# Two sets of recurrence scratch tiles, and channel chains issued in alternation

## The chip, the cores and the metric

The kernel runs on the 8 cores of one Trainium2 chip, one batch element per core, with no exchange between cores. Each core has five engines that take their own instruction streams in order and meet at semaphores: TensorE (PE), VectorE (DVE), ScalarE (ACT), GpSimd (POOL) and SyncE (SP, here only DMA issue). The metric is the device time of the slowest core in microseconds.

## The reference, cut to what matters

One hybrid decoder layer on x (8, 4096, 1024), float32. The change lies in the recurrent half of the mixer, `rg_lru` with the convolution before it:

```python
h = rms_norm(x, norm_mix)
x_rnn, gate_rnn, q, k, v = split(h @ w_in)           # 512 columns each
x_rnn = causal_depthwise_conv(x_rnn, conv_w, conv_b)  # width 4
r = sigmoid(einsum('bshi,hij->bshj', xh, w_a) + b_a)  # xh: x_rnn in 8 heads of 64
i = sigmoid(einsum('bshi,hij->bshj', xh, w_x) + b_x)
a = exp(-8 * r * softplus(-lam))
b = sqrt(1 - a * a) * (i * x_rnn)
hidden[t] = a[t] * hidden[t - 1] + b[t]               # scan over the sequence
y_rnn = hidden * gelu(gate_rnn)
y_sb = stick_breaking_attention(q, k, v)              # causal, 8 heads of 64
x = x + concat(rms_norm(y_rnn), rms_norm(y_sb)) @ w_out
```

After it come a cross-attention into 256 memory tokens and a mixture of 16 experts; the change does not touch them.

## The kernel before

**Stages.** The program has three stages with a barrier between them: the mixer (to about 2890 us), the cross-attention and the experts. Only the mixer's code changes.

**Tiles.** The mixer works on 8 query tiles of 512 tokens. For each tile `front_ops(qt)` (line 477) norms and transposes the tokens into `hT`, projects them with `w_in` in ten blocks of 256 columns (q, k, v, gate, and last blocks 0 and 1, the recurrence's input), and runs the recurrence. `attention(qt)` (line 590) goes through 8 heads times the key blocks of 128 up to the tile, one *item* each: 32 items for tile 0, 64 for tile 1, up to 256 for tile 7. `back_ops(qt)` (line 559) norms the attention output and applies `w_out`.

**An attention item.** Its steps are pipelined by hand: `s0` computes the scores Z of item t+2 on TensorE, `s1` takes e = exp(Z) and sp = ln(e + 1) of item t+1 on ScalarE, `s3` adds two matmuls to Z of item t (with the triangle `negU` on sp, and with `negOnes` on R, the running sum of the sp before) and lets VectorE update R with sp, `s4` takes w = exp(Z) on ScalarE, `s5` multiplies w of item t-1 with V. There are 3 buffers for Z (PSUM), sp and w. So each item's last matmul needs VectorE's R update of the item before, and w needs that matmul.

**What sets the order.** `front_ops` and `back_ops` only record their instructions (`Defer`, line 243). `attention(qt)` then issues, behind each item's steps, an equal share of a side list: `back_ops(qt - 1)`, `front_ops(qt + 1)` and six weight conversions by DMA (lines 670 to 673). With 35 steps in tile 0 and 259 in tile 7, that is about 11.7 side instructions a step in tile 0 and 2.3 in tile 6. `front_ops(0)` is issued alone ahead of everything. Every engine takes its instructions strictly in the order issued.

**A chain.** Each of blocks 0 and 1 holds two *chains* of 128 channels (lines 517 to 551), four per front, c = 0 to 3, one behind the other. A chain has 37 instructions: 8 matmuls into a PSUM bank, the convolution on VectorE (halo copy from `hal`, copy `xrt`, one tensor_scalar and three scalar_tensor_tensor into `xc`, halo saved, cast `xcb`), a matmul and a sigmoid for r, a matmul and a sigmoid for the input gate `ig`, then b and a by exponentials and a logarithm on ScalarE, two products, the scan with its state in `hst`, the product with the gate `gg`, the square `sq`, a matmul with ones, and the addition into `rstdF`. The sigmoid of the fronts 0 to 3 is three ScalarE passes; that of the fronts 4 to 7 is one ScalarE pass, an addition and a reciprocal on VectorE (`sigmoid_from`, line 468).

**Buffers.** All four chains use the same scratch tiles `xrt`, `xc`, `r_`, `ig`, `b_`, `xcb` (lines 408 to 410). The PSUM banks of the small matmuls and projections come in turn from `pmR`, two banks: within a chain they alternate, so that the two gate matmuls go to different banks. `xhR` has 3 buffers for the residual tokens that `back_ops` loads (line 580), adds to (line 585) and stores (line 586); load and store stand in SyncE's queue in this order, item by item.

## Time and profile before

| | us |
|---|---|
| median of 6 runs (5534.08 to 5628.45) | 5574.36 |
| the profiled execution | 5532.07 |
| its span on the slowest core | 5530.6 |
| ScalarE busy in the span | 2856.0 |
| TensorE busy (matmuls) | 3750.5 |
| VectorE busy | 2039.6 |

The page of the profile gives shares over the whole program, which mixes three stages with different limits. The change is in the first, so the rows below are cut from that stage: busy time of each engine by stretch, the timeline of single instructions, and who waited for whom. In a stretch, the span less an engine's busy time is its idle time. In a timeline row the first number is the start, the second how long it took; "x3" means that three like instructions are merged, from the first start to the last end.

### The profile page before, as it was taken

The numbers are of one execution on the slowest core, as the hardware profiler recorded it, in microseconds if no ns is written. First come the engines' busy times: TensorE is split into PE (matmuls) and PEld (weight loads), VectorE is DVE, ScalarE is ACT, GpSimd is POOL, SyncE is SP. The second block draws the span as 40 slices with busy tenths as digits, with TensorE's granted clock in tenths as the row PEclk, the third lists the DMA queues.
The fourth block names the chain that finished last, engine by engine and source line by source line (L and its number), as shares of the span: only waits on it lengthen the run. The fifth ranks groups of instructions, "written<-read, shape, count | busy, mean of one in ns | idle before, by whom it ended". The sixth has DMA issues, their size and how long they took to land. (4 is left out here: it accounts for less than half of the span.)

```text
span 5530.6 us, 64662 instructions; the slowest of 8 cores (5509.6 to 5530.6 us)
## 1 busy us (share of the span) xinstructions
PE 3750.5 (68%) x16080; PEld 1509.3 (27%) x16080; DVE 2039.6 (37%) x4139; ACT 2856.0 (52%) x5222; POOL 469.4 (8%) x463
## 2 busy tenths in 40 slices
PE   3545656667577667665544656647887977879798
PEld 1212222223122122211112222213333333333343
DVE  4434343443633633532222333333333333333332
ACT  2546676768788889889952232212323233232322
POOL 1000000000000000000000000001121111211121
PEclk8767778879789789889986767668999999999999
DMA  5634333422223122100224212123343243432443
GB/s 78 82 64 59 77 46 69 54 56 33 35 62 43 20 62 35 20 5 12 39 61 94 80 58 84 54 93 125 137 146 135 82 156 128 143 134 82 156 139 118
DMA packets 245839, 436.01 MB, mean 79 GB/s; under 512 B 15088, under 2 KB 146160, under 8 KB 245488
## 3 DMA queue, kind: packets, MB, share of 16 engines
q1 hardware_dynamic: 102672, 339.29, 18.3%
q0 software_dynamic: 142816, 92.59, 13.7%
q8 instruction: 153, 2.51, 0.2%
q14 instruction: 198, 1.62, 0.1%
HBM read 474.07 MB, written 75.50 MB: 99 GB/s over the span
## 5 line engine op out<-in xcount | busy, mean ns | idle before, releaser
L181 ACT ACTIVATE sp_u<-e__u,cst_u 128x512 bf16<-128x512 f32 (+3 forms) x1152 | 790.4, 686 | 166.8 <-ACT e__u L181 5.9
L184 PE MATMUL Z_u<-qT_u,KT_u 128*128 128x512 bf16 (+3 forms) x1152 | 456.9, 397 | 598.6 <-ACT w_u L181 590.2
L197 DVE TENSOR_TENSOR R_u<-R_u,sp_u 128x512 bf16<-128x512 bf16 (+2 forms) x1088 | 433.3, 398 | 1134.8 <-PE Z_u L184 1079.3
L181 ACT ACTIVATE w_u<-Z_u 128x512 bf16<-128x512 f32 (+3 forms) x1152 | 629.4, 546 | 250.7 <-PE Z_u L184 248.1
L181 ACT ACTIVATE e__u<-Z_u 128x512 f32<-128x512 f32 (+3 forms) x1152 | 636.3, 552 | 20.4 <-PE Z_u L184 20.2
L184 PE MATMUL g_u<-tT_u,wg_u 128*128 128x512 bf16 x2048 | 536.4, 403 | 137.2 <-DMA wg_u<-wg_s 84.9
L181 ACT ACT_TABLE_LOAD x212 | 272.0, 1283 | 604.0 <-DVE rt_u L201 215.4
L184 PE MATMUL u_u<-tT_u,wu_u 128*128 128x512 bf16 x2048 | 522.8, 397 | 2.1
L184 PE MATMUL Z_u<-R_u,negOnes_u 128*128 128x512 bf16 (+1 forms) x1088 | 446.5, 410 | 62.6 <-DVE R_u L197 62.6
L184 PE MATMUL Z_u<-sp_u,negU_u 128*128 128x512 bf16 (+3 forms) x1152 | 462.2, 401 | 15.6 <-ACT sp_u L181 15.3
L184 PE MATMUL dn_u<-wd_u,hid_u 128*128 128x512 bf16 x2048 | 455.9, 381 | 21.8 <-DVE hid_u L197 17.6
L184 PE MATMUL O_u<-w_u,V_u 128*128 128x512 bf16 (+3 forms) x1152 | 460.2, 400 | 6.8 <-ACT w_u L181 1.9
L197 DVE TENSOR_TENSOR hid_u<-u_u,sg_u 128x512 bf16<-128x512 f32 x256 | 177.1, 692 | 675.6 <-POOL sg_u L197 504.4
L181 ACT ACTIVATE sg_u<-g_u 128x512 f32<-128x512 f32 x256 | 152.6, 597 | 519.0 <-PE g_u L184 484.0
L197 POOL TENSOR_TENSOR sg_u<-sg_u,cb_u 128x512 f32<-128x512 f32 x256 | 295.3, 1154 | 1440.5 <-ACT sg_u L181 1401.3
L184 PEld LDWEIGHTS Z_u<-qT_u,KT_u 128*128 128x128 bf16 x1152 | 114.2, 99 | 1028.0 <-issue 1015.8
L188 PE MATMUL pT_u<-ident_u,hn_u 128*128 128x128 bf16 x784 | 147.1, 273 | 355.6 <-DVE hn_u L208 336.9
L184 PEld LDWEIGHTS g_u<-tT_u,wg_u 128*128 128x128 bf16 x2048 | 194.6, 101 | 387.9 <-issue 201.4
L184 PE MATMUL pm_u<-hT_u,win_u 128*128 128x512 bf16 x1024 | 295.2, 408 | 2.1 <-DVE hT_u L194 2.0
L184 PEld LDWEIGHTS u_u<-tT_u,wu_u 128*128 128x128 bf16 x2048 | 202.2, 102 | 250.0 <-issue 48.8
L184 PEld LDWEIGHTS dn_u<-wd_u,hid_u 128*128 128x128 bf16 x2048 | 192.8, 98 | 255.2 <-issue 36.3
L188 PEld LDWEIGHTS pT_u<-ident_u,hn_u 128*128 128x128 bf16 x784 | 79.3, 120 | 478.0 <-issue 465.4
(159 smaller groups left out, 4158.0 us busy)
## 6 DMA issues: line engine op xcount, KB each, us to landing
wg_u<-wg_s SPq DMA_DIRECT2D x128, 512.0 KB, 3.8
wu_u<-wu_s SPq DMA_DIRECT2D x128, 512.0 KB, 5.1
wd_u<-wd_s SPq DMA_DIRECT2D x128, 512.0 KB, 6.0
win_u<-w_in POOLq DMA_DIRECT2D x80, 512.0 KB, 7.5
xs_u<-x SPq DMA_DIRECT2D x32, 512.0 KB, 4.2
xh_u<-x SPq DMA_DIRECT2D x64, 256.0 KB, 3.6
wo_u<-w_out POOLq DMA_DIRECT2D x16, 1024.0 KB, 25.0
x1s<-xh_u SPq DMA_DIRECT2D x64, 256.0 KB, 2.5
```

The lines of the kernel that those rows point to most:

```text
L181: self.S.op("act", lambda e: e.activation(out=out, in_=in_, func=func, **kw), reads, writes)
L184: self.S.op("pe", lambda e: e.matmul(out, lhsT=lhsT, rhs=rhs, start=start, stop=stop, skip_group_check=skip), reads, writes, inc=inc)
L188: self.S.op("pe", lambda e: e.transpose(out=out, in_=in_, identity=ident), reads, writes, inc=inc)
L197: self.S.op(eng, lambda e: e.tensor_tensor(out=out, in0=in0, in1=in1, op=op), reads, writes)
```

## The change

The scratch tiles get a second set (`LT`, two dictionaries of tiles), and to make room `xhR` falls from 3 buffers to 2. The marks that order the accesses to `hal` and `hst` are kept per chain rather than one for all. The chain's code moves into a function `lru_chain`, which takes a set of scratch tiles and one PSUM bank and uses this bank for all its matmuls. For blocks 0 and 1, `front_ops` records the two chains of the block in two lists, one with each set and bank, and then appends their instructions in alternation. Each chain has the same 37 instructions as before, the side list is as long as before, and all that stands ahead of and behind the chains keeps its place in it.

```diff
@@ -403,13 +403,20 @@
             winR = Rot([sb("win%d" % i, [128, 8, 256], BF16) for i in range(4)], "win")
             woR = Rot([sb("wo%d" % i, [128, 8, 512], BF16) for i in range(2)], "wo")
             xsR = Rot([sb("xs%d" % i, [128, D], F32) for i in range(2)], "xs")
-            xhR = Rot([sb("xh%d" % i, [128, 512], F32) for i in range(3)], "xh")
+            xhR = Rot([sb("xh%d" % i, [128, 512], F32) for i in range(2)], "xh")
             t512 = lambda n, d, c: Rot([sb("%s%d" % (n, i), [128, 512], d) for i in range(c)], n)
-            xrt = sb("xrt", [128, 515], F32)
-            xc, r_, ig, b_ = [sb(n, [128, 512], F32) for n in ("xc", "r_", "ig", "b_")]
-            xcb = sb("xcb", [128, 512], BF16)
+            LT = []
+            for i in range(2):
+                T = {"xrt": sb("xrt%d" % i, [128, 515], F32), "xcb": sb("xcb%d" % i, [128, 512], BF16)}
+                for n_ in ("xc", "r_", "ig", "b_"):
+                    T[n_] = sb("%s%d" % (n_, i), [128, 512], F32)
+                for n_ in ("xrtB", "xcB", "rB", "igB", "bB", "xcbB"):
+                    T[n_] = Buf("%s%d" % (n_, i))
+                LT.append(T)
             e_ = sb("e_", [128, 512], F32)
-            xrtB, xcB, rB, igB, bB, xcbB, eB = [Buf(n) for n in ("xrt", "xc", "r", "ig", "b", "xcb", "e")]
+            eB = Buf("e")
+            halBs = [Buf("hal%d" % i) for i in range(4)]
+            hstBs = [Buf("hst%d" % i) for i in range(4)]
             sqR = t512("sq", BF16, 2)
             spR = t512("sp", BF16, 3)
             wR = t512("w", BF16, 3)
@@ -425,8 +432,8 @@
-            k.memset("pool", hal[:], 0.0, [halB])
-            k.memset("pool", hst[:], 0.0, [hstB])
+            k.memset("pool", hal[:], 0.0, halBs)
+            k.memset("pool", hst[:], 0.0, hstBs)
@@ -473,6 +480,45 @@
+
+            def lru_chain(kk, qt, c, wt, wtB, lo, T, bank, yTt, yTB):
+                pa, paB = bank
+                for dc in range(8):
+                    kk.mm(pa[:, :], wt[:, dc, lo:lo + 128], hT[:, dc, :], dc == 0, dc == 7,
+                          [wtB, hTB], [paB], inc=(dc == 7))
+                kk.copy("dve", T["xrt"][:, 0:3], hal[:, c, 0:3], [halBs[c]], [T["xrtB"]])
+                kk.copy("dve", T["xrt"][:, 3:515], pa[:, :], [paB], [T["xrtB"]])
+                kk.ts("dve", T["xc"][:], T["xrt"][:, 0:512], pp[:, c * 4:c * 4 + 1], pp[:, 16 + c:17 + c],
+                     ALU.mult, ALU.add, [T["xrtB"], ppB], [T["xcB"]])
+                for t in range(1, 4):
+                    kk.stt(T["xc"][:], T["xrt"][:, t:t + 512], pp[:, c * 4 + t:c * 4 + t + 1], T["xc"][:],
+                          ALU.mult, ALU.add, [T["xrtB"], ppB, T["xcB"]], [T["xcB"]])
+                kk.copy("dve", hal[:, c, 0:3], T["xrt"][:, 512:515], [T["xrtB"]], [halBs[c]])
+                kk.copy("dve", T["xcb"][:], T["xc"][:], [T["xcB"]], [T["xcbB"]])
+                pg, pgB = bank
+                kk.mm(pg[:, :], wbd[:, c, :], T["xcb"][:], True, True, [wbdB, T["xcbB"]], [pgB], inc=True)
+                sigmoid_from(kk, T["r_"], T["rB"], pg, pgB, c12[:, 12 + c:13 + c], on_act=(qt <= 3))
+                pg2, pg2B = bank
+                kk.mm(pg2[:, :], wbd[:, 4 + c, :], T["xcb"][:], True, True, [wbdB, T["xcbB"]], [pg2B], inc=True)
+                sigmoid_from(kk, T["ig"], T["igB"], pg2, pg2B, c12[:, 16 + c:17 + c], on_act=(qt <= 3))
+                kk.act(T["b_"][:], T["r_"][:], AF.Exp, [T["rB"], constB], [T["bB"]], scale=c12[:, 8 + c:9 + c])
+                kk.act(T["r_"][:], T["r_"][:], AF.Exp, [T["rB"], constB], [T["rB"]], scale=c12[:, 4 + c:5 + c])
+                kk.ts("dve", T["b_"][:], T["b_"][:], -1.0, 1.0, ALU.mult, ALU.add, [T["bB"]], [T["bB"]])
+                kk.act(T["b_"][:], T["b_"][:], AF.Ln, [T["bB"], constB], [T["bB"]], bias=cst[:, 1:2])
+                kk.act(T["b_"][:], T["b_"][:], AF.Exp, [T["bB"]], [T["bB"]], scale=0.5)
+                kk.tt("dve", T["ig"][:], T["ig"][:], T["xc"][:], ALU.mult, [T["igB"], T["xcB"]], [T["igB"]])
+                kk.tt("dve", T["b_"][:], T["b_"][:], T["ig"][:], ALU.mult, [T["bB"], T["igB"]], [T["bB"]])
+                kk.scan(T["xc"][:], T["r_"][:], T["b_"][:], hst[:, c:c + 1], [T["rB"], T["bB"], hstBs[c], T["xcB"]], [T["xcB"]])
+                kk.copy("dve", hst[:, c:c + 1], T["xc"][:, 511:512], [T["xcB"]], [hstBs[c]])
+                kk.tt("dve", yTt[:, c, :], T["xc"][:], gg[:, c, :], ALU.mult, [T["xcB"], ggB], [yTB])
+                sq, sqB = sqR.next()
+                kk.tt("dve", sq[:], yTt[:, c, :], yTt[:, c, :], ALU.mult, [yTB], [sqB])
+                ps_, psB_ = bank
+                kk.mm(ps_[:, :], ones[:], sq[:], True, True, [constB, sqB], [psB_], inc=True)
+                if c == 0:
+                    kk.copy("dve", rstdF[:], ps_[:, :], [psB_], [rstdFB])
+                else:
+                    kk.tt("dve", rstdF[:], ps_[:, :], rstdF[:], ALU.add, [psB_, rstdFB], [rstdFB])
@@ -496,6 +542,18 @@
+                    if b in (0, 1):
+                        chains = []
+                        for half in range(2):
+                            cops = []
+                            lru_chain(Defer(k, S, cops), qt, b * 2 + half, wt, wtB, half * 128, LT[half],
+                                      (pmR.t[half], pmR.b[half]), yTt, yTB)
+                            chains.append(cops)
+                        for i in range(max(len(chains[0]), len(chains[1]))):
+                            for cops in chains:
+                                if i < len(cops):
+                                    ops.append(cops[i])
+                        continue
@@ -514,41 +572,6 @@
-                        else:
-                            c = b * 2 + half
-                            kk.copy("dve", xrt[:, 0:3], hal[:, c, 0:3], [halB], [xrtB])
-                            kk.copy("dve", xrt[:, 3:515], pa[:, :], [paB], [xrtB])
...
-                            kk.copy("dve", hal[:, c, 0:3], xrt[:, 512:515], [xrtB], [halB])
-                            kk.copy("dve", xcb[:], xc[:], [xcB], [xcbB])
-                            pg, pgB = pmR.next()
-                            kk.mm(pg[:, :], wbd[:, c, :], xcb[:], True, True, [wbdB, xcbB], [pgB], inc=True)
-                            sigmoid_from(kk, r_, rB, pg, pgB, c12[:, 12 + c:13 + c], on_act=(qt <= 3))
...
-                            kk.tt("dve", yTt[:, c, :], xc[:], gg[:, c, :], ALU.mult, [xcB, ggB], [yTB])
-                            sq, sqB = sqR.next()
-                            kk.tt("dve", sq[:], yTt[:, c, :], yTt[:, c, :], ALU.mult, [yTB], [sqB])
-                            ps_, psB_ = pmR.next()
-                            kk.mm(ps_[:, :], ones[:], sq[:], True, True, [constB, sqB], [psB_], inc=True)
-                            if c == 0:
-                                kk.copy("dve", rstdF[:], ps_[:, :], [psB_], [rstdFB])
-                            else:
-                                kk.tt("dve", rstdF[:], ps_[:, :], rstdF[:], ALU.add, [psB_, rstdFB], [rstdFB])
```

What this moves is shown at three places. The first is on VectorE in front 0, the convolution at the start of the first two chains. Before, one chain:

```order
L194 COPY xrt_u36<-pm0_u53 128x512
L204 TENSOR_SCALAR xc_u37<-xrt_u36,pp_u9 128x512
L208 SCALAR_TENSOR_TENSOR xc_u37<-xrt_u36,pp_u9,xc_u37 128x512 x3
L194 COPY hal_u15<-xrt_u36 128x3
L194 CAST xcb_u41<-xc_u37 128x512
L204 TENSOR_SCALAR b__u40<-b__u40 128x512
```

and now two, with the numbers 0 and 1 for the two sets:

```order
L194 COPY xrt0_u35<-pm0_u58 128x512
L194 COPY xrt1_u41<-pm1_u59 128x512
L204 TENSOR_SCALAR xc0_u37<-xrt0_u35,pp_u9 128x512
L204 TENSOR_SCALAR xc1_u43<-xrt1_u41,pp_u9 128x512
L208 SCALAR_TENSOR_TENSOR xc0_u37<-xrt0_u35,pp_u9,xc0_u37 128x512
L208 SCALAR_TENSOR_TENSOR xc1_u43<-xrt1_u41,pp_u9,xc1_u43 128x512
```

Between two instructions of one chain there is now one of the other. The second place is on VectorE during tile 4, in the last chain or pair of front 5, around the sigmoids; R is attention's running sum. Before:

```order
L197 TENSOR_TENSOR R1_u52<-R1_u52,sp0_u45 128x512
L201 TENSOR_SCALAR r__u38<-r__u38 128x512
L222 RECIPROCAL r__u38<-r__u38 128x512
L197 TENSOR_TENSOR R1_u52<-R1_u52,sp1_u46 128x512
L201 TENSOR_SCALAR ig_u39<-ig_u39 128x512
L197 TENSOR_TENSOR R1_u52<-R1_u52,sp2_u47 128x512
L222 RECIPROCAL ig_u39<-ig_u39 128x512
L197 TENSOR_TENSOR R1_u52<-R1_u52,sp0_u45 128x512
```

and now:

```order
L201 TENSOR_SCALAR r_0_u38<-r_0_u38 128x512
L201 TENSOR_SCALAR r_1_u44<-r_1_u44 128x512
L197 TENSOR_TENSOR R1_u57<-R1_u57,sp1_u51 128x512
L222 RECIPROCAL r_0_u38<-r_0_u38 128x512
L222 RECIPROCAL r_1_u44<-r_1_u44 128x512
L197 TENSOR_TENSOR R1_u57<-R1_u57,sp2_u52 128x512
L197 TENSOR_TENSOR R1_u57<-R1_u57,sp0_u50 128x512
L201 TENSOR_SCALAR ig0_u39<-ig0_u39 128x512
L201 TENSOR_SCALAR ig1_u45<-ig1_u45 128x512
L222 RECIPROCAL ig0_u39<-ig0_u39 128x512
L222 RECIPROCAL ig1_u45<-ig1_u45 128x512
```

Where an R update stood behind each reciprocal, two reciprocals now stand ahead of one. The third place is on TensorE in front 0, from the end of the first chain (now: the first pair) to the matmuls of the next. Before:

```order
L184 MATMUL pm1_u54<-xcb_u41,wbd_u11 128x512
L184 MATMUL pm0_u53<-xcb_u41,wbd_u11 128x512
L184 MATMUL pm1_u54<-sq0_u43,ones_u4 128x512
L184 MATMUL pm0_u53<-hT_u18,win0_u25 128x512 x8
L184 MATMUL pm1_u54<-xcb_u41,wbd_u11 128x512
```

and now:

```order
L184 MATMUL pm0_u58<-xcb0_u36,wbd_u11 128x512
L184 MATMUL pm1_u59<-xcb1_u42,wbd_u11 128x512
L184 MATMUL pm0_u58<-xcb0_u36,wbd_u11 128x512
L184 MATMUL pm1_u59<-xcb1_u42,wbd_u11 128x512
L184 MATMUL pm0_u58<-sq0_u48,ones_u4 128x512
L184 MATMUL pm1_u59<-sq1_u49,ones_u4 128x512
L184 MATMUL pm0_u58<-hT_u18,win1_u26 128x512
L184 MATMUL pm1_u59<-hT_u18,win1_u26 128x512
```

Before, the matmuls behind a square went to the other bank; now the next pair's go to the two banks that have just taken the squares. The streams of SyncE and GpSimd are the same before and after.

## Rows read from the trace of the kernel before

**Rows 1.** The page's first line: the span.

```profile
span 5530.6 us, 64662 instructions; the slowest of 8 cores (5509.6 to 5530.6 us)
```

**Rows 2.** Stretches: us, PE, PEld, DVE, ACT, POOL busy (instructions), PEclk, DMA share, GB/s.

```profile
71.50:158.40 86.90, 17.19 (x43) 4.95 (x41) 38.82 (x68) 34.98 (x55) 2.39 (x3) 0.59 0.23 26
...
221.30:311.60 90.30, 28.23 (x88) 10.82 (x88) 43.27 (x80) 45.33 (x82) 4.77 (x6) 0.59 0.56 63
...
465.50:560.90 95.40, 37.59 (x113) 12.54 (x111) 45.42 (x86) 52.84 (x95) 0.00 (x0) 0.64 0.34 41
...
733.10:837.60 104.50, 50.90 (x155) 16.50 (x153) 48.81 (x96) 69.20 (x124) 0.00 (x0) 0.66 0.31 37
...
1041.70:1157.90 116.20, 66.40 (x191) 20.07 (x191) 80.34 (x121) 76.98 (x137) 0.00 (x0) 0.67 0.26 33
...
2236.40:2373.20 136.80, 87.01 (x297) 26.02 (x297) 90.76 (x148) 121.96 (x218) 0.00 (x0) 0.83 0.00 1
2373.20:2843.00 469.80, 282.07 (x1121) 91.65 (x1120) 121.48 (x282) 423.00 (x773) 6.64 (x8) 0.97 0.13 21
```

**Rows 3.** Timeline of front 0, second chain: start, duration, engine, line, out<-in, count [idle before].

```profile
90.97 3.62 PE L184 MATMUL pm_u<-hT_u,win_u 128*128 128x512 bf16 x8
...
94.76 0.69 DVE L194 COPY xrt_u<-pm_u 128x512 f32<-128x512 f32 x1 [2.72 <-PE pm_u L184]
...
96.33 2.46 DVE L208 SCALAR_TENSOR_TENSOR xc_u<-xrt_u,pp_u,xc_u 128x512 f32<-128x512 f32 x3
...
98.89 0.43 DVE L194 CAST xcb_u<-xc_u 128x512 bf16<-128x512 f32 x1
...
99.57 1.01 PE L184 MATMUL pm_u<-xcb_u,wbd_u 128*128 128x512 bf16 x2 [4.99 <-DVE xcb_u L194]
100.31 0.69 ACT L181 ACTIVATE r__u<-pm_u,c_u 128x512 f32<-128x512 f32 x1 [13.72 <-PE pm_u L184]
101.09 0.72 ACT L181 ACTIVATE r__u<-r__u,cst_u 128x512 f32<-128x512 f32 x1
101.90 0.63 ACT L181 ACTIVATE r__u<-r__u 128x512 f32<-128x512 f32 x1
102.44 0.67 ACT L181 ACTIVATE ig_u<-pm_u,c_u 128x512 f32<-128x512 f32 x1
...
106.77 0.63 ACT L181 ACTIVATE b__u<-b__u 128x512 f32<-128x512 f32 x1
107.57 0.69 DVE L197 TENSOR_TENSOR b__u<-b__u,ig_u 128x512 f32<-128x512 f32 x1 [1.19 <-ACT b__u L181]
...
110.61 0.42 DVE L197 TENSOR_TENSOR sq_u<-yT_u 128x512 bf16<-128x512 bf16 x1
...
111.39 0.58 PE L184 MATMUL pm_u<-sq_u,ones_u 128*128 128x512 bf16 x1 [10.81 <-DVE sq_u L197]
...
111.77 3.48 PE L184 MATMUL pm_u<-hT_u,win_u 128*128 128x512 bf16 x8
112.09 0.69 DVE L197 TENSOR_TENSOR rstdF_u<-pm_u,rstdF_u 128x512 f32<-128x512 f32 x1 [1.05 <-PE pm_u L184]
```

**Rows 4.** Timeline during tile 6: a reciprocal, the R behind it, the next w.

```profile
2245.32 3.35 DVE L222 RECIPROCAL r__u<-r__u 128x512 f32<-128x512 f32 x1
2248.59 0.36 DVE L197 TENSOR_TENSOR R_u<-R_u,sp_u 128x512 bf16<-128x512 bf16 x1
...
2250.44 0.60 ACT L181 ACTIVATE w_u<-Z_u 128x512 bf16<-128x512 f32 x1
```

**Rows 5.** Who waited for whom, ScalarE, 1041.7 to 1157.9: us, times, longest.

```profile
ACT b__u L181 <- DVE b__u L204: 5.9, 4, 2.0
ACT b__u L181 <- DVE r__u L222: 4.8, 3, 1.7
```

**Rows 6.** The stores to `x1s` in the tile's view: issue to landing.

```profile
DMA to landing us min/median/max: 2.0/2.5/8.9
```

17 lines of the change are left out of this document (removed).

## The prediction

> **What bounds the kernel now.** I began with the span, 5530.6 us [rows 1], and then cut the first half of it into stretches: those in which the four recurrence chains of a front are issued, and one stretch with attention alone [rows 2]. The reader should look at ScalarE's column. With attention alone ScalarE works 423.00 of 469.80 us, so it is the bound there, and an attention item costs about 1.8 us (256 items). In the chain stretches it is not: it is idle 51.9, 45.0, 42.6, 35.3 and 39.2 us in the first five (span less ScalarE's busy time), and 14.8 us of 136.8 in the last shown. No other engine is full either; in the second stretch VectorE has 43.27 and TensorE 28.23 of 90.3 us. Work that no engine bounds is bound by order: each instruction of a chain waits for the one before it. The timeline of one chain without attention shows it [rows 3]: 8 matmuls, then VectorE alone, then ScalarE alone, then VectorE alone, 20.8 us from 90.97 to 111.77, when the next chain's matmuls start. So chains set the pace of the early fronts, and ScalarE more and more of the late ones.
>
> **What the change does to a pair of chains.** It issues chain 0's first instruction, chain 1's first, chain 0's second, and so on. Both chains are therefore in the same phase at the same time, on the same engine. TensorE's, VectorE's and ScalarE's work isn't laid beside each other; it is done twice in each phase. I expect no halving, but three smaller gains.
>
> *(a) Waits inside an engine.* Two instructions of which the second needs the first have a gap: ScalarE starts the second r pass at 101.09, 0.78 after the first, which takes 0.69; three such passes of VectorE take 2.46, or 0.855 each, for 0.75 of work. Without a dependence the next starts before the end: ig at 102.44, 0.54 after a pass of 0.63 [rows 3], and VectorE's R at 2248.59, while the reciprocal from 2245.32 ends at 2248.67 [rows 4]. That is 0.18 us for each. I count 6 such places on ScalarE and 7 on VectorE in a chain; with another chain's instruction between them they close: 13 x 0.18 = 2.3 per chain, 4.7 per pair, 9.4 per front of four.
>
> The Trainium skill, "VectorE: DVE Perf Modes", section "The DRAIN you can't avoid", says otherwise: chained VectorE operations take the same time with a semaphore after each as with one at the end. By that rule (a) would be nothing on VectorE; the rows above disagree by 0.18 us per place, and I go by the rows, with the rule as a rival below.
>
> *(b) Handovers.* Between engines a chain loses 0.17 (matmuls end at 94.59, VectorE starts at 94.76), 0.25 and 0.74 (cast ends at 99.32, small matmuls at 99.57, ScalarE at 100.31), 0.17 (107.40 to 107.57), 0.36 and 0.38 (square ends at 111.03, its matmul at 111.39, the next chain at 111.77) [rows 3]: 2.1 us, paid once per pair where it was paid twice: 4.2 per front. And at three handovers the next engine can start on chain 0 while the last instruction of chain 1 still runs, worth one instruction each (0.35 + 0.53 + 0.34, durations less the overlap): 1.2 per pair, 2.4 per front.
>
> *(c) What it adds.* A chain now keeps one PSUM bank for all its matmuls. So the second pair's matmuls wait until VectorE has added both squares: the add after the square's matmul runs from 112.09 to 112.78 [rows 3], two of them end near 113.4, where the old order would start at 112.15: 1.3 us. The first pair waits for the last gate copy (about 0.9), and the front's end has two adds in a row (0.6). Together 2.8 per front. That the second gate matmul waits for ScalarE's read of the first costs nothing: ScalarE needs two more passes of each chain before it wants it.
>
> For the first front, which runs alone, (a) + (b) - (c) is 9.4 + 4.2 + 2.4 - 2.8 = **13.2 us**. In the next three, attention's own instructions already stand in some of the gaps. ScalarE's counts give the items: (82 - 42) / 3 = 13, (95 - 42) / 3 = 18 and (124 - 42) / 3 = 27, where 42 are the chains' own [rows 2]. An item closes about one gap on each of two engines, 26, 35 and all of the 52; so of the 9.4 there are left 4.7, 3.0 and 0, and the fronts gain **8.5, 6.8 and 3.8**.
>
> The last four fronts (during tiles 3 to 6) take the sigmoid with a reciprocal on VectorE: 3.35 us each [rows 4], two per chain. In the new order two stand back to back in 10 of the 16 places (the second piece of order shows two); in the other 6 an R update of attention falls between. R is what attention waits for: TensorE's next matmul reads it, and ScalarE's w reads that. A single reciprocal just fits: R at 2248.59, w at 2250.44, hardly late. With a second one R would start 3.27 later, at 2251.86, 1.4 after that w; with R's 0.36 and a matmul, w is about 2.3 late. The bounds are 0 (ScalarE still has other work in its queue) and 3.35; I take 2.3, as it comes from the very place. 10 x 2.3 = 23, less the 20 single ones of before at about 0.4 each (the idle time that the late stretch shows is little more), leaves a loss of 15. Against it, ScalarE now waits for its own chain: 5.9 us in 4 waits for the step before the logarithm, 4.8 in 3 for the reciprocal, in the first of these stretches [rows 5]; with the other chain's passes between, I take 70% of it back, 7.5. In the last stretch there is almost nothing to win: 14.8 us idle, of which attention alone would leave 64 x 0.18 = 11.7 (46.8 idle over 256 items). I take 5 and 2 for the two stretches between, and 1 for the last: 15.5. The late fronts come to **0**, with 3 to 4 us won at tile 3 and as much lost at tile 6.
>
> Four buffers become two sets: no instruction is added, and none of SyncE's or GpSimd's moves. The residual buffers fall from 3 to 2, so a load waits for the store two back rather than three. It stands in SyncE's queue behind the last store anyway, which waits for 8 matmuls (3.5 us) and an add; a store lands after 2.5 us in the median [rows 6]. I take 0; at the slowest landing, 8.9 us, one load would be some 4 us late, and I allow 5 in all. The matmuls of the chains run at 0.44 us each (8 in 3.5) [rows 3], TensorE's lower clock, with 0.59 granted in the early stretches [rows 2]; longer phases without matmuls won't raise it, and I leave it as it is.
>
> **Sum.** 13.2 + 8.5 + 6.8 + 3.8 + 0 = 32.3 us less. The profiled execution took 5532.07 us, span and start together: 5532 - 32 = **5500**. That execution lies 42 us under the median of the six runs shown, 5574.36; a median over such a mix would be about 5542.
>
> **The rivals.**
> - *The chains really overlap*, so that a pair takes little more than one chain. Then half of ScalarE's idle time in the first four stretches goes: (51.9 + 45.0 + 42.6 + 35.3) / 2 = 87, and the time is 5445. For it: no engine is over half busy there. Against it: lockstep brings both chains to the same engine at once, and ScalarE's part of a pair alone is 2 x 7.1 us (100.31 to 107.40).
> - *Little changes*: the gaps in an engine stay although the chains alternate. Then (a), 9.4 + 4.7 + 3.0 = 17, is lost, and the time is 5517. That is also what comes out (5519) if attention fills every gap and only the first front gains. By the rule of the skill named above this is the outcome; the trace so far speaks against it.
> - *Slower*: VectorE's blocks become twice as long and attention waits behind them. Price: 10 reciprocals at the full 3.35, 33.5; and the convolution, 94.76 to 99.32 or 4.6 us per chain [rows 3], in one block of twice the length, 8 late pairs x 4.6 = 37. Less 22 that the first two fronts still gain, 5581. It decides only if attention has no slack at all; the R that was hardly late behind 3.35 us says that it has about that much.
>
> **Chances.** Forecast 0.56, real overlap 0.20, little change 0.16, slower 0.08. One per cent is 55 us, about what a measurement can tell from no change here: faster by more takes the overlap and the top of the forecast, 0.22; slower by more takes the worst half of the last, 0.05; within it 0.73. The likeliest case alone spans 5480 to 5515. The range takes in the overlap, 5445, and at the top the loss and a median that lies higher than the profiled execution, 5575.
>
> **What would show it.** Right: chains of the first front start in pairs some 34 us apart instead of 2 x 20.8; passes of 0.75 on VectorE follow each other at about 0.67; the stretches of the first fronts shrink by 13, 9, 7 and 4 us; behind two reciprocals R and w come about 2 us late in the last two of the late stretches. Wrong: a pair takes under 30 us (overlap), the pitch stays at 0.85 (little change), or the late stretches grow by more than 10 us each (slower).

## The result, and the profile after

The changed kernel takes 5490.82 us in the median of 10 runs, the kernel before 5581.53 in 20 runs beside it; over the comparable runs the ratio is **0.9828**, 95% interval 0.9772 to 0.9885. That is a gain of 1.7%, faster by the bound of one per cent that the prediction named, an outcome to which it gave 0.22. By the interval it is 64 to 126 us of 5532; the mixers of the two profiled executions differ by 60.5, about twice the 32 us forecast, and what follows goes by these. (In some executions the cores of one die show a lower granted clock and take longer: the ratios leave these out, the medians don't, and for the two kernels marked with a star, profiled in such an execution, the table takes the cores of the other die.)

Where the gain lies is read from the mixer in pieces. VectorE clears R at the start of every head, 64 times, so these instructions mark where the front ahead of everything ends and each tile begins. The view of this line in the changed kernel (times, durations, first and last start):

```profile
L212 DVE MEMSET R_u<- x64: 485/485/485, 143.3 to 2713.8; 128x512 bf16 x64
```

Front 0 ends at 143.3 on this core. The table gives such pieces for all kernels of this study, each as the median over the cores, in us: front 0 up to the first of these starts, a tile from the start of its first head to the copy of its last head's output out of PSUM, and the mixer as a whole. Tile n holds front n + 1.

| kernel | front 0 | tile 0 | 1 | 2 | 3 | 4 | 5 | 6 | mixer | ratio to before |
|---|---|---|---|---|---|---|---|---|---|---|
| before | 159.4 | 148.2 | 243.6 | 276.6 | 319.6 | 356.6 | 403.2 | 453.0 | 2884.5 | 1 |
| changed | 142.5 | 133.1 | 232.0 | 268.4 | 306.9 | 353.7 | 404.9 | 458.5 | 2824.0 | 0.9828 |
| two sets, not alternated (`seq2`) | 160.4 | 149.7 | 239.1 | 276.6 | 319.4 | 355.3 | 401.6 | 456.3 | 2879.9 | none |
| waits put back (`gap`) | 151.4 | 142.4 | 235.4 | 273.1 | 312.6 | 359.5 | 408.4 | 463.5 | 2869.2 | 0.999 |
| early fronts only (`early`) | 142.7 | 132.9 | 232.0 | 266.6 | 320.7 | 355.0 | 402.8 | 456.0 | 2835.3 | 0.9858 |
| half a chain apart (`stagger`) | 141.5 | 130.5 | 229.4 | 265.9 | 306.6 | 353.9 | 397.4 | 456.5 | 2800.5 | 0.9846 |
| squares in one bank (`sqbank`)* | 139.0 | 135.8 | 224.2 | 261.1 | 307.8 | 352.4 | 411.2 | 456.8 | 2806.8 | 0.9884 |
| pipeline (`pipe`) | 131.7 | 125.1 | 217.4 | 256.0 | 307.6 | 351.4 | 399.9 | 460.0 | 2770.0 | 0.9791 |
| two instructions apart, late (`lag`) | 141.8 | 132.9 | 228.6 | 266.3 | 303.1 | 348.1 | 392.3 | 450.0 | 2785.7 | 0.9817 |
| four apart, late (`lag4`)* | 142.3 | 133.1 | 227.1 | 266.4 | 303.2 | 352.4 | 398.3 | 454.3 | 2801.9 | 0.982 |
| pipeline early, two apart late (`both`) | 129.6 | 120.9 | 217.2 | 253.6 | 304.7 | 347.6 | 392.5 | 449.2 | 2735.4 | 0.9743 |

How fine this is: the early fronts of `lag` are word for word those of the changed kernel, and differ from them by 0.7, 0.2, 3.4 and 2.1 us. So in tiles 1 and 2 some 3.5 us say nothing. The intervals of the ratios of `early`, `stagger`, `sqbank`, `pipe`, `lag`, `lag4` and `both` all overlap that of the changed kernel; what sets these kernels apart is read from the pieces, of one profiled execution each.

From before to the changed kernel the mixer lost 60.5 us: 16.9 in front 0, 15.1, 11.6 and 8.2 in the next three tiles, 12.7 and 2.9 in tiles 3 and 4; tiles 5 and 6 grew by 1.6 and 5.5. The stages behind the mixer moved by 3 and 1 us. The same stretches as [rows 2] but the last, in the changed kernel (us, busy time of PE, PEld, DVE, ACT, POOL with instructions, granted clock, DMA share, GB/s):

```profile
74.20:142.50 68.30, 15.47 (x41) 4.40 (x39) 35.55 (x66) 30.82 (x54) 1.75 (x2) 0.56 0.25 29
207.00:281.00 74.00, 24.61 (x82) 8.62 (x81) 40.75 (x80) 41.25 (x80) 3.30 (x4) 0.60 0.67 76
433.00:516.00 83.00, 36.69 (x114) 11.88 (x112) 43.36 (x88) 50.72 (x95) 0.00 (x0) 0.62 0.42 47
690.00:785.50 95.50, 51.39 (x153) 15.99 (x151) 46.66 (x97) 67.63 (x124) 0.00 (x0) 0.64 0.34 39
988.00:1092.50 104.50, 64.53 (x192) 18.78 (x190) 78.88 (x123) 76.44 (x138) 0.00 (x0) 0.69 0.30 37
2170.00:2309.50 139.50, 90.79 (x285) 25.85 (x284) 88.53 (x148) 119.00 (x213) 0.00 (x0) 0.77 0.00 1
```

ScalarE does the same work in fewer us: its idle time in the first five falls from 51.9, 45.0, 42.6, 35.3 and 39.2 us to 37.5, 32.8, 32.3, 27.9 and 28.1, while the sixth rises from 14.8 to 20.5. No stretch is full yet.

The second pair of chains in front 0, which answers [rows 3] (timeline: start, duration, engine, line, out<-in, count, idle before):

```profile
102.14 0.76 DVE L197 TENSOR_TENSOR sq_u<-yT_u 128x512 bf16<-128x512 bf16 x2
102.93 1.01 PE L184 MATMUL pm_u<-sq_u,ones_u 128*128 128x512 bf16 x2 [15.50 <-DVE sq_u L197]
...
103.62 0.69 DVE L194 COPY rstdF_u<-pm_u 128x512 f32<-128x512 f32 x1 [0.71 <-PE pm_u L184]
...
104.56 0.58 PE L184 MATMUL pm_u<-hT_u,win_u 128*128 128x512 bf16 x1 [0.62 <-DVE rstdF_u L194]
...
105.36 5.31 PE L184 MATMUL pm_u<-hT_u,win_u 128*128 128x512 bf16 x14 [0.21 <-DVE xrt_u L194]
...
110.82 0.38 PE L184 MATMUL pm_u<-hT_u,win_u 128*128 128x512 bf16 x1
110.84 1.29 DVE L194 COPY xrt_u<-pm_u 128x512 f32<-128x512 f32 x2 [5.59 <-PE pm_u L184]
...
113.21 4.05 DVE L208 SCALAR_TENSOR_TENSOR xc_u<-xrt_u,pp_u,xc_u 128x512 f32<-128x512 f32 x6
...
117.32 0.75 DVE L194 CAST xcb_u<-xc_u 128x512 bf16<-128x512 f32 x2
...
118.62 1.27 ACT L181 ACTIVATE r_u<-pm_u,c_u 128x512 f32<-128x512 f32 x2 [21.55 <-PE pm_u L184]
...
119.78 1.33 ACT L181 ACTIVATE r_u<-r_u,cst_u 128x512 f32<-128x512 f32 x2
...
129.11 1.15 ACT L181 ACTIVATE b_u<-b_u 128x512 f32<-128x512 f32 x2
129.91 1.29 DVE L197 TENSOR_TENSOR b_u<-b_u,ig_u 128x512 f32<-128x512 f32 x2 [1.41 <-ACT b_u L181]
...
135.33 0.76 DVE L197 TENSOR_TENSOR sq_u<-yT_u 128x512 bf16<-128x512 bf16 x2
...
136.81 1.49 DVE L197 TENSOR_TENSOR rstdF_u<-pm_u,rstdF_u 128x512 f32<-128x512 f32 x2 [0.72 <-PE pm_u L184]
```

The first three rows are the end of the pair before. From the copies to `xrt` on, every row counts the instructions of both chains, two of a kind (six convolution passes). A pair takes 33.2 us (103.62, when the pair before adds its first square, to 136.81); the forecast was 34. Six convolution passes take 4.05, so 0.66 from one to the next (4.05 less one pass of 0.75, by 5).

### The profile page after: what moved, and what is told of

The parts are those of the page before. It is cut to its first block and busy times, and to the rows that moved or that the text cites. A ratio compares the mean times of both kernels' runs of the same rounds, so it can differ in the third digit from the quotient of the medians.

```text
span 5492.6 us, 64737 instructions; the slowest of 8 cores (5430.2 to 5492.6 us)
## 1 busy us (share of the span) xinstructions
PE 3771.0 (69%) x16080; PEld 1509.2 (27%) x16080; DVE 2022.5 (37%) x4139; ACT 2844.4 (52%) x5222; POOL 469.5 (9%) x463
## 5 line engine op out<-in xcount | busy, mean ns | idle before, releaser
L184 PE MATMUL Z_u<-qT_u,KT_u 128*128 128x512 bf16 (+3 forms) x1152 | 456.5, 396 | 594.9 <-ACT w_u L181 586.5
L184 PE MATMUL g_u<-tT_u,wg_u 128*128 128x512 bf16 x2048 | 548.7, 410 | 136.2 <-DMA wg_u<-wg_s 84.4
L184 PEld LDWEIGHTS g_u<-tT_u,wg_u 128*128 128x128 bf16 x2048 | 197.2, 102 | 396.8 <-issue 239.1
L184 PE MATMUL pm_u<-hT_u,win_u 128*128 128x512 bf16 x1024 | 284.2, 396 | 9.3 <-DVE rstdF_u L194 2.8
## 6 DMA issues: line engine op xcount, KB each, us to landing
xh_u<-x SPq DMA_DIRECT2D x64, 256.0 KB, 3.4
x1s<-xh_u SPq DMA_DIRECT2D x64, 256.0 KB, 2.3
```

Source lines behind the costliest of these rows:

```text
L184: self.S.op("pe", lambda e: e.matmul(out, lhsT=lhsT, rhs=rhs, start=start, stop=stop, skip_group_check=skip), reads, writes, inc=inc)
```

## The experiments

Three theories stood against each other. **A**: the alternation closes the gaps between dependent instructions of one engine and pays handovers once per pair. **B**: the second set of tiles itself does it, since one chain may start while the other still holds its tiles. **C**: a wait on the own engine costs nothing, and the gain is handovers and overlap alone. The later runs ask how the parts of the sum were mis-sized, and what a better order gives.

### Two sets, chains one behind the other (`seq2`)

```diff
-                        for i in range(max(len(chains[0]), len(chains[1]))):
-                            for cops in chains:
-                                if i < len(cops):
-                                    ops.append(cops[i])
+                        for cops in chains:
+                            ops.extend(cops)
```

> Two sets of scratch tiles, one PSUM bank per chain, two residual buffers, all as in the changed kernel, but the two chains of a block one behind the other instead of in alternation. Theory A (the alternation closes gaps inside an engine and shares handovers): nothing is closed or shared, so every tile of the mixer is back at the times of before within 2 us (front 0 at 159, tile 0 at 148, tile 1 at 244, tile 2 at 277, tile 3 at 320) and the whole is at 5532, or some 5 us above it because the second gate matmul now waits for a read of the first. Rival B (it is the second set of tiles that frees the chains): at least half of the 60 us that the mixer lost stays lost, about 5500 or less.

Measured: 5567.81 us in the median of 4 runs, 5585.65 before it (13 runs); no ratio was formed from so few. The mixer takes 2879.9, against 2884.5, and all pieces stand within 5 us of before. So B falls: two sets without the alternation bring no more than that, where the changed kernel gained 60.5. Nor can more of a cost be seen from the residual buffers, which are two here as well (tile 6 is 3.3 longer, the others no more than 1.5).

### The waits put back (`gap`)

The changed kernel's order, but each of the 8 VectorE and 6 ScalarE instructions of an early front's chain (10 and 2 in a late front's) that depend on the one before them in the chain also waits for the instruction that stands directly ahead in the recurrence's stream of its engine, which is mostly the other chain's.

```diff
+            eng = {"act": "act", "mm": "pe", "stt": "dve", "scan": "dve", "recip": "dve"}.get(name) or a[0]
+            mark = self._marks.pop(0) if eng != "pe" else False
...
+                if mark:
+                    S.extra = (toks[eng],)
```

> The changed kernel's order, banks and buffers, but each of the 8 VectorE and 6 ScalarE instructions of a chain that needed its predecessor on its own engine now waits for whatever chain instruction stands just ahead of it on that engine, so that the gap of 0.18 us comes back while the handovers stay shared. Theory A: 14 x 0.18 x 4 = 10 us come back in front 0 (142.5 to 152), and by the prediction's discount for attention's instructions 5, 3 and 0 in tiles 0 to 2; if the gaps are not filled by attention at all, 10 in each of tiles 0 to 3. Rival C (a wait on the own engine costs nothing, the gain is in handovers and overlap alone): no tile changes by more than 2 us.

Measured: ratio 0.999, 0.9937 to 1.0043, which can't be told from no change; the mixer got back 45.2 of the 60.5 us. Against the changed kernel front 0 grew by 8.9, tiles 0 to 6 by 9.3, 3.4, 4.7, 5.7, 5.8, 3.5 and 5.0: 46 us for waits alone, with no computing instruction added or moved. The timeline of the second pair in front 0 of this kernel (same columns):

```profile
117.33 5.04 DVE L211 SCALAR_TENSOR_TENSOR xc_u<-xrt_u,pp_u,xc_u 128x512 f32<-128x512 f32 x6
...
125.35 1.54 ACT L184 ACTIVATE r_u<-r_u,cst_u 128x512 f32<-128x512 f32 x2
```

The six convolution passes take 5.04 instead of 4.05, the two exponentials 1.54 instead of 1.33: 0.2 us for each wait. C falls. What is left between `seq2` and `gap`, the handovers less what the banks cost, is 9.0 in front 0 and 7.3, 3.7, 3.5 and 6.8 in tiles 0 to 3; in tiles 4 to 6 it is a loss, 4.2, 6.8 and 7.2.

### Alternation in the early fronts only (`early`)

```diff
+                        if qt > 3:
+                            chains = [chains[0] + chains[1], []]
```

> Alternation in fronts 0 to 3 only; in fronts 4 to 7 (those with reciprocals, issued during tiles 3 to 6) the two chains stand one behind the other. Theory of the prediction (late fronts come to nothing): tiles 3 to 6 together as in the changed kernel within 5 us. What the trace of the changed kernel says: tile 3 goes back up by 12 us and tile 4 by 3, tile 5 down by 2 and tile 6 by 5, 8 us more in sum; 5475 against 5467 for the changed kernel.

Measured: ratio 0.9858, 0.9792 to 0.9925. Tile 3 took back 13.8 us, tile 4 1.3; tiles 5 and 6 got 2.1 and 2.5 shorter. So the alternation of the late fronts brings about 10 us, not the 0 within 5 of the forecast, and nearly all in tile 3, where the prediction had put 3 to 4; it costs little in the last two. Of the 5.5 us by which tile 6 grew, 3 stand here and in `seq2` too (456.0 and 456.3 against 453.0), where the late fronts aren't alternated. They come with what these kernels share with the changed one, the second set of tiles, one bank for a chain and two residual buffers; which of these it is was not tried.

### Four chains, half a chain apart (`stagger`)

`held` are the four chains of a front; `merged(a, b)` spreads the instructions of b evenly among those of a.

```diff
+                            ops.extend(held[0][:16])
+                            for c in range(4):
+                                nxt = held[c + 1][:16] if c < 3 else []
+                                ops.extend(merged(held[c][16:29], nxt))
+                                ops.extend(held[c][29:])
```

> The four chains of a front run half a chain apart with the same two sets and banks: the gate and exponential part of a chain is merged with the projection and convolution of the next one, its tail follows. If engine phases laid beside each other are worth more than closed gaps: a chain of front 0 takes about 12.4 us (tail 4.0, projection 3.8, convolution 4.6) against 16.6 in alternation and 20.8 before, front 0 ends at 127 instead of 142, tiles 0 to 2 gain 5 to 10 us each on the changed kernel, and the late tiles lose their double reciprocals, 5 to 8 us; 5430 to 5440 in all. If attention's own chain sets the pace of tiles 1 to 6 whatever the order of the side work: only front 0 gains, 15 us.

Measured: ratio 0.9846, 0.9736 to 0.9955, and front 0 only 1 us shorter than in the changed kernel, where 15 were expected. Tiles 0 to 2 are 2.5 to 2.6 shorter (5 to 10 expected), tile 5 7.5, the mixer 23.5. The timeline of its front 0 tells why (two chains, 15.1 us apart):

```profile
91.72 0.58 PE L184 MATMUL pm_u<-sq_u,ones_u 128*128 128x512 bf16 x1 [9.65 <-DVE sq_u L197]
92.10 0.63 PE L184 MATMUL pm_u<-xcb_u,wbd_u 128*128 128x512 bf16 x1
...
92.83 0.69 ACT L181 ACTIVATE r_u<-pm_u,c_u 128x512 f32<-128x512 f32 x1 [5.96 <-PE pm_u L184]
...
106.83 0.58 PE L184 MATMUL pm_u<-sq_u,ones_u 128*128 128x512 bf16 x1 [9.18 <-DVE sq_u L197]
```

TensorE takes its instructions in order, and the next chain's gate matmul (`wbd`) stands behind this chain's matmul on the square. That one waits 9.65 us for the end of the chain; only then may the gate matmul go and ScalarE begin, after 5.96 us of nothing. So the rows put the lost overlap down to one matmul's place in a queue; `pipe`, below, moves it.

### The pair's squares in one bank (`sqbank`)

```diff
-                ps_, psB_ = bank
-                kk.mm(ps_[:, :], ones[:], sq[:], True, True, [constB, sqB], [psB_], inc=True)
+                ps_, psB_ = sbank
+                kk.mm(ps_[:, :], ones[:], sq[:], c % 2 == 0, c % 2 == 1, [constB, sqB], [psB_], inc=True)
...
+                            ob = half ^ b
...
+                        ops.extend(chains[0][:8] + chains[1][:8])
```

This alters three things: TensorE adds up the two squares of a pair, so that one addition on VectorE falls away; the next pair's first chain (`ob`) uses the other bank; and the projection matmuls go chain by chain.

> The changed kernel with one alteration at the chain's end: the two squares of a pair are summed by TensorE in one bank (one addition on VectorE instead of two), the next pair's first chain uses the other bank, and the 8+8 projection matmuls go chain by chain rather than in alternation. It measures term (c) of the forecast, the waits for banks and the added additions, put at 2.8 us a front. If (c) was that large: front 0 shorter by about 3 us (1.3 for the next pair, 0.6 for the addition at the end, and up to 1.2 since chain 0's convolution starts 8 matmuls earlier), the next three fronts 1 to 3 each; total 5 to 10 us less than the changed kernel. If (c) cost next to nothing: front 0 within 1 us of the changed kernel, total within 5.

Measured: ratio 0.9884, 0.9839 to 0.993; front 0 3.5 us shorter than in the changed kernel, tile 0 2.7 and tile 5 6.3 longer, tiles 1 and 2 7 to 8 shorter. In front 0, which runs alone, that fits a term (c) of 2.8, but it doesn't isolate it: up to 1.2 of the 3 expected were for the projections' order. As a whole the pieces and the runs disagree: the mixer is 17.2 us shorter than in the changed kernel, the ratio no better. What made tile 0 and tile 5 longer was not tried.

### The pipeline (`pipe`)

```diff
+                            sk = half if b == 1 and half == 1 else 1 - half
...
+                            ops.extend(P[0] + DV[0] + merged(G[0] + E[0], P[1] + DV[1]))
+                            for c in range(4):
+                                ops.extend(merged(T1[c], G[c + 1] + P[c + 2]))
+                                ops.extend(T2[c])
+                                ops.extend(merged(E[c + 1], DV[c + 2]) if E[c + 1] else [])
```

P are a chain's 8 projection matmuls, DV the convolution, G the gates, E the exponentials, T1 the products and the square, T2 the square's matmul and its addition; `sk` is the bank of the square's matmul.

> The four chains of a front are cut into pieces and issued as a pipeline: the gate matmuls and sigmoids of chain c+1 and the projection of chain c+2 stand between the last products of chain c, the exponentials of chain c+1 between the convolution of chain c+2. The square's matmul goes to the other chain's bank, so that the projection of the next but one chain need not wait for it. Nothing is computed otherwise. Theory 'order, not engines': what the run with chains half a chain apart could not show is that its overlap was blocked by TensorE's order (the next gate matmul stood behind the square's matmul of the chain before, pitch 15.0 us a chain in front 0). With that undone ScalarE (7.1 us a chain) and VectorE (about 8) are the next bounds: pitch about 9 to 10 a chain, front 0 some 18 to 22 us shorter than in the changed kernel, the next two tiles 3 to 8 shorter, late tiles as in the run half a chain apart; total 5430 to 5460 by profile. Theory 'lockstep has got what there is': pitch stays at 15 or more in front 0, total within 15 us of the changed kernel. A third outcome: front 0 shorter, later tiles not, because attention's instructions stand between the pieces and hold TensorE's and VectorE's order instead; then total 5450 to 5475.

Measured: ratio 0.9791, 0.9726 to 0.9855. Front 0 is 10.8 us shorter than in the changed kernel, where 18 to 22 were expected, and tiles 0 to 2 8.0, 14.6 and 12.4, more than I expected there; tiles 3 to 6 change by no more than 5. A chain takes 12 us rather than 9 to 10. Its timeline is read from the kernel `both`, whose early fronts are the same:

```profile
89.22 0.69 ACT L181 ACTIVATE r_u<-pm_u,c_u 128x512 f32<-128x512 f32 x1 [1.44 <-PE pm_u L184]
...
90.43 3.62 PE L184 MATMUL pm_u<-hT_u,win_u 128*128 128x512 bf16 x8
...
92.03 0.42 DVE L197 TENSOR_TENSOR sq_u<-yT_u 128x512 bf16<-128x512 bf16 x1
...
93.84 0.63 PE L184 MATMUL pm_u<-sq_u,ones_u 128*128 128x512 bf16 x1
...
94.58 0.69 DVE L194 COPY rstdF_u<-pm_u 128x512 f32<-128x512 f32 x1 [2.13 <-PE pm_u L184]
...
95.45 0.69 DVE L194 COPY xrt_u<-pm_u 128x512 f32<-128x512 f32 x1
...
100.96 0.69 ACT L181 ACTIVATE r_u<-pm_u,c_u 128x512 f32<-128x512 f32 x1 [2.30 <-PE pm_u L184]
```

Now the next chain's sigmoids start 11.74 us after the last (89.22, 100.96), and ScalarE waits 1.44 and 2.30 us in place of 13.72 [rows 3]. What is left is again an order: the square is ready at 92.45, its matmul stands behind 8 projection matmuls until 93.84, and VectorE waits 2.13 us for it with the next convolution queued behind.

### Two instructions apart in the late fronts (`lag`), and four (`lag4`)

```diff
+                        lag = 0 if qt <= 3 else 2
+                        for i in range(37 + lag):
+                            for cops, j in ((chains[0], i), (chains[1], i - lag)):
+                                if 0 <= j < len(cops):
+                                    ops.append(cops[j])
```

> The changed kernel, but in the last four fronts (tiles 3 to 6) the second chain of a pair is issued two instructions behind the first, so that no two of the four reciprocals of a pair stand next to each other in the chains' order. If two reciprocals back to back cost attention what the forecast said (2.3 us each time, ten times), tiles 3 to 6 get shorter, above all 5 and 6, which had grown by 1.6 and 5.5 us: together 10 to 20 us less than the changed kernel, with the first three tiles unchanged. If the doubled reciprocal is not what makes tile 6 longer: tiles 5 and 6 within 2 us of the changed kernel. If the gain of tile 3 (12.7) came from the lockstep of like instructions, it falls; if from the gaps closed by any other instruction in between, it stays within 2 us.

Measured: ratio 0.9817, 0.9732 to 0.9902. Tiles 3 to 6 are 3.8, 5.6, 12.6 and 8.5 us shorter than in the changed kernel, 30 in all. The two fastest of its 4 runs took 5431.13 and 5440.39 us, the five fastest of the changed kernel's 10 took 5454.99 to 5471.94. Two reciprocals of the changed kernel in tile 6, to be held against [rows 4], and below them two of `lag`:

```profile
2262.67 0.42 DVE L197 TENSOR_TENSOR R_u<-R_u,sp_u 128x512 bf16<-128x512 bf16 x1 [1.90 <-PE Z_u L184]
...
2263.01 6.56 DVE L222 RECIPROCAL r_u<-r_u 128x512 f32<-128x512 f32 x2
...
2269.49 0.36 DVE L197 TENSOR_TENSOR R_u<-R_u,sp_u 128x512 bf16<-128x512 bf16 x1
2270.47 0.60 ACT L181 ACTIVATE w_u<-Z_u 128x512 bf16<-128x512 f32 x1 [2.44 <-PE Z_u L184]
2270.48 0.42 DVE L197 TENSOR_TENSOR R_u<-R_u,sp_u 128x512 bf16<-128x512 bf16 x1 [0.63 <-PE Z_u L184]
...
2272.76 0.42 DVE L197 TENSOR_TENSOR R_u<-R_u,sp_u 128x512 bf16<-128x512 bf16 x1 [1.51 <-PE Z_u L184]
```

```profile
2171.16 0.36 DVE L197 TENSOR_TENSOR R_u<-R_u,sp_u 128x384 bf16<-128x384 bf16 x1 [0.86 <-PE Z_u L184]
2171.43 3.35 DVE L222 RECIPROCAL r_u<-r_u 128x512 f32<-128x512 f32 x1
...
2174.70 0.36 DVE L197 TENSOR_TENSOR R_u<-R_u,sp_u 128x512 bf16<-128x512 bf16 x1
...
2175.69 0.42 DVE L197 TENSOR_TENSOR R_u<-R_u,sp_u 128x512 bf16<-128x512 bf16 x1 [0.30 <-PE Z_u L184]
2176.03 3.34 DVE L222 RECIPROCAL r_u<-r_u 128x512 f32<-128x512 f32 x1
...
2179.30 0.36 DVE L197 TENSOR_TENSOR R_u<-R_u,sp_u 128x512 bf16<-128x512 bf16 x1
...
2180.28 0.42 DVE L197 TENSOR_TENSOR R_u<-R_u,sp_u 128x512 bf16<-128x512 bf16 x1 [0.30 <-PE Z_u L184]
```

Attention needs one R per item, and with attention alone an item takes 1.84 us (469.80 for 256 items, [rows 2]). In the changed kernel the three items from 2262.67 to 2272.76 take 10.1 us instead of 5.5, a loss of 4.6, and ScalarE stands idle for 2.44 us before a w. In `lag` two R updates pass between one reciprocal and the next, and the four items from 2171.16 to 2180.28 take 9.1 instead of 7.4, a loss of 1.8 for two reciprocals. Each figure is of one place.

A distance of two also covers handovers better, so it isn't proof of the reciprocals by itself. The run with `lag = 4` was made to tell: there the second chain's reciprocal for r meets the first chain's for the input gate again, once per pair.

> As the run with the second chain two instructions behind in the last four fronts, but four behind. Then one of the three spacings between a pair's four reciprocals closes again: the second chain's reciprocal for r and the first chain's for the input gate stand next to each other or with one instruction between, once per pair (in the changed kernel twice, two behind: never). If doubled reciprocals are what made tiles 4 to 6 longer, about half of what the distance of two gained there comes back: tiles 5 and 6 some 4 to 7 us each longer than at a distance of two. If it is the distance as such that gains (more of the two chains' handovers covered, reciprocals without weight): tiles 4 to 6 within 2 us of the distance of two, or shorter.

Measured: ratio 0.982, 0.9738 to 0.9902. Tiles 4, 5 and 6 are 4.3, 6.0 and 4.3 us longer than at a distance of two: 14.6 of the 26.7 us that two had won there, about half, for half of the meetings. The meeting, in this kernel's timeline (core 2):

```profile
2173.11 3.35 DVE L222 RECIPROCAL ig_u<-ig_u 128x512 f32<-128x512 f32 x1
...
2176.37 3.29 DVE L222 RECIPROCAL r_u<-r_u 128x512 f32<-128x512 f32 x1
2179.59 0.36 DVE L197 TENSOR_TENSOR R_u<-R_u,sp_u 128x512 bf16<-128x512 bf16 x1
```

So what `lag` gains in the late tiles comes from the doubled reciprocals, not from the distance as such.

### Both orders together (`both`)

The pipeline where the sigmoid is ScalarE's (front 0 and tiles 0 to 2), the distance of two where it has reciprocals (tiles 3 to 6).

> The pipelined order for the first four fronts (front 0 and tiles 0 to 2) and, for the last four (tiles 3 to 6), pairs in alternation with the second chain two instructions behind. If the gains lie in separate stretches and add up: against the changed kernel front 0 -11, tiles 0 to 2 -8, -14 and -12, tiles 3 to 6 -4, -6, -12 and -8, in all some 70 to 76 us, total 5380 to 5400, about 15 to 20 below the run with pipelined order throughout. If an early gain is given back later (by the state in which tile 3 begins, by the weights' transfers that no longer come in time): less than 50 of it, total above 5410.

Measured: ratio **0.9743**, 0.9678 to 0.9808. Against the changed kernel front 0 is 12.9 us shorter, tiles 0 to 2 12.2, 14.8 and 14.8, tiles 3 to 6 2.2, 6.1, 12.4 and 9.3; the mixer 88.6 less, more than the 70 to 76 expected. The gains add, and nothing is given back later. It is the fastest kernel of the study by its mixer, which takes 149 us less than before, with the same instructions in another order, a second set of tiles, and the square's matmul in the other chain's bank.

## Why the prediction was right and wrong

**The mechanism was right.** The predicted signs came: a pair in 33.2 us (34), a pitch of 0.66 on VectorE (0.67), the stretches of the first fronts shorter in falling order, tile 3 shorter and tile 6 longer, w late behind two reciprocals. Rival "little changes" fell with `gap`. By `gap` the waits cost 46 us over the mixer, and six convolution passes of VectorE 5.04 us with them against 4.05 without; the places were 14 in an early chain, one more than I had counted. The rival leaned on a sentence of the Trainium skill, "VectorE: DVE Perf Modes", section "The DRAIN you can't avoid": in its measurement of eight copies a semaphore after each cost nothing extra. For the instructions here that does not hold. The same section of the Trainium skill adds that a next operation which isn't held starts earlier. With that the trace agrees, 0.66 from pass to pass against 0.86 in [rows 3]. "Real overlap" was no description of this change, a pair takes 33 us and not under 30. What it promised for front 0 and tiles 0 to 2, 87 us, was there to be had by another order: `both` is 106.5 shorter than before in these four.

**That 5490.82 stands so near the forecast 5500 is partly luck.** 5500 was meant for an execution like the profiled one; for a median over a mix of executions the prediction named 5542, and against that the result is 51 us lower. The profiled execution of the changed kernel, 5494.09, comes near 5500 because its slowest core, with 5492.6 us, lies 25 above the median of its cores (5467.2), where before it was 10 (5530.6 and 5520.8). The mixers say how far off the sum was: 60.5 for 32.3.

**Front 0 was about right**: 16.9 us for 13.2, per pair 8.4 (2 x 20.8 less 33.2) for 6.6. From [rows 3] and the rows of the changed kernel: from the copy to the cast's end 4.56 per chain before, 9.12 for two, and 7.23 for the pair now; ScalarE's part twice 7.09, now 11.64; from the first product to the square twice 3.46, now 6.18. These are the gaps, 5.2 us where (a) had 4.7. From the cast to ScalarE the two chains lost 2.0, the pair 0.6; from ScalarE to VectorE 0.3, now 0.35 of overlap: 2.1 for the 2.0 that were forecast. The rest, 1.1, lies in the way from the square's end to the next copy, where the forecast's gains and bank waits about cancelled: 4.53 per chain (111.03 to 111.77, 90.97 to 94.76), 9.06 for two, and 7.94 for the pair (102.90 to 110.84). The wait for the banks was smaller than I had it, as the next matmul starts at 104.56, 0.9 after two squares would have let it go (102.93 and twice 0.38), not 1.3; and VectorE begins to copy at 110.84 while the pair's last matmul still runs (to 111.20), an overlap that I hadn't counted.

**The step that failed is the discount for attention.** I took an attention item to close about one gap on each engine and struck 4.7, 6.4 and 9.4 us of (a) in tiles 0, 1 and 2. `gap` gives the (a) that was there: 9.3, 3.4 and 4.7, against 4.7, 3.0 and 0. In tile 0 nothing was to be struck, in tile 2 about half; tile 1 is right within what the pieces can tell. I had spread the 13 or 27 items evenly over a chain's gaps. In tile 0 some 12 instructions of the side list follow each item in a row, so most gaps have no attention instruction near them; that is by the count, no run tests it. The handovers came to 7.3, 3.7 and 3.5 against 3.8 each, only tile 0 off. Together 34.9 us for the 19.1 forecast; the undiscounted 13.2 for each, 39.6, would have been closer.

**The late fronts were right in sign and pattern, wrong in size on both sides.** The loss by doubled reciprocals was put at 23 gross, 15 net of the single ones; removing it gave 30 (`lag`), or 1.9 for each of the 16 places where two stand close together. A pair of singles loses 1.8 (by the rows of `lag`) where I had 0.8, a double 4.6 where I had 2.3. The gain was put at 15.5; without the doubles it is 39 (before to `lag`: 16.5, 8.5, 10.9 and 3.0 in tiles 3 to 6). So the two errors nearly cancelled, 8.5 us gained where I said 0. Of the 23 us of gain that I missed, 9 each lie in tile 3 (16.5 for 7.5) and in tile 5 (10.9 for 2). ScalarE's waits in tile 3 (us, times, longest), first w's before, beside [rows 5], then the two longest of the changed kernel, whose only other row is 0.7 us for `e_`:

```profile
ACT w_u L181 <- PE Z_u L184: 17.5, 14, 3.1
```

```profile
ACT w_u L181 <- PE Z_u L184: 18.5, 20, 1.9
ACT r_u L181 <- PE pm_u L184: 2.2, 1, 2.2
```

The waits for `b` of [rows 5], 10.7 us, are gone altogether rather than by 70%; and w waits about as long in tile 3 as it did, so the doubled reciprocals cost little there (3.8 by `lag`). The same for w in the last stretch, tile 6, before and in the changed kernel:

```profile
ACT w_u L181 <- PE Z_u L184: 3.0, 9, 0.6
```

```profile
ACT w_u L181 <- PE Z_u L184: 10.7, 17, 3.6
```

There w's waits rose to 10.7 from 3.0.

**Put at nothing, and nothing to be seen**: the residual buffers, two instead of three, though `seq2` can't part them from the 3 us in tile 6. **Borne out in front 0 but not isolated, open elsewhere**: (c), by `sqbank`.

## What to carry to other kernels

Where no engine is full, two chains in alternation earn what stands between dependent instructions of one engine, here 0.2 us each, and it is worth counting these; other work in the same stream need not close such gaps (in tile 0 it closed none that `gap` shows), so don't discount them without looking at where it is issued. Lockstep brings like instructions together, which is right for short ones and wrong for the one long instruction that somebody else waits behind: two places of distance were worth 30 us here. And before a staggered order is called useless, look at each in-order queue for the one instruction that puts the overlap back in line. The Trainium skill says in "Perfetto Trace Analysis", section "Optimization Strategy", that a kernel whose most-contended engine changes over time may gain by interleaving such regimes. `pipe` agrees, with 10.8 us in front 0 on top of the alternation's 16.9.

## What the runs showed of the hardware

I had left TensorE's clock as it was. A pair's 16 projection matmuls now stand in one block, and the clock rises within it. Stretches of the second pair's block in the changed kernel, then of the third chain's 8 and of the end of the fourth's before (same columns as above, the granted clock third from the end):

```profile
104.50:109.40 4.90, 4.63 (x11) 1.61 (x12) 0.75 (x3) 0.00 (x0) 0.00 (x0) 0.50 0.00 0
109.40:111.30 1.90, 1.64 (x6) 0.44 (x4) 0.46 (x1) 0.00 (x0) 0.00 (x0) 0.92 0.00 0
```

```profile
111.70:115.50 3.80, 3.56 (x9) 1.10 (x8) 0.83 (x3) 0.00 (x0) 0.00 (x0) 0.57 0.00 0
134.90:136.10 1.20, 1.09 (x4) 0.29 (x2) 0.00 (x0) 0.00 (x0) 0.00 (x0) 0.76 0.00 0
```

0.50 of full speed is 1.2 GHz; behind some eleven matmuls with hardly a pause the stretch shows 0.92, most of it at 2.4 GHz. It earned next to nothing: the block takes 6.6 us (104.56 to 111.20), and the two blocks of 8 that it replaces took 6.7, 3.48 from 111.77 and 3.23 from 132.76, as the clock rose at the end of the second of them too (0.76).
